# Mixer norms of a two-layer trunk: x turned by f32 matmuls with a diagonal of inverse roots, and first weights split in quarters

## The reference

```python
def rms_norm(x, gain):
    return x * lax.rsqrt(jnp.mean(x * x, axis=-1, keepdims=True) + EPS) * gain

for l in range(2):
    h = rms_norm(x, norm_mix[l])
    if l == 0:
        p = h @ even_w_in          # 1024 x 2560: u, v (gated), q, k, vv (attention)
        mix = concat(gated(u, v), stick_breaking(q, k, vv)) @ even_w_out
    else:
        mix = (B * conv3(C * hh)) @ odd_w_out    # B, C, hh: h @ odd_w_in, 1024 x 3072
    x = x + mix
    x = x + experts(rms_norm(x, norm_ffn[l]))    # 32 experts, 2 of them for each token
return rms_norm(x, norm_final)
```

## Time and profile before

| | |
|---|---|
| median of 3 runs | 1137.8 us (1137.17, 1137.8, 1138.01) |
| profiled execution | 1137.29 us, span 1135.5 us |
| busy: PE, DVE, ACT | 853.1 us (75%), 281.2 us (25%), 199.0 us (18%) |
| mean granted PE clock | 0.896 of full |
| DMA | 438.56 MB, 386 GB/s over the span |

### The profile page before, as it was taken

How to read it: one execution, slowest core, us unless ns; L and a number is a source line. 1 busy time by engine, 2 the same in 40 slices (tenths; PEclk the granted TensorE clock), 3 DMA queues, 4 the chain that set the end, 5 groups by cost and what they waited for, 6 DMA issues and landing times.

```text
span 1135.5 us, 29778 instructions
## 1 busy us (share of the span) xinstructions
PE 853.1 (75%) x13613; PEld 697.3 (61%) x13614; DVE 281.2 (25%) x692; ACT 199.0 (18%) x372; POOL 5.2 (0%) x31
## 2 busy tenths in 40 slices
PE   5999798576677676787679998876666776676874
PEld 5888776355555455565479987755554555554652
DVE  5666521011011010111157634110110110110211
ACT  5574310000000000000163331010000000000101
POOL 1000000000000000000000000000000000000000
PEclk9999899989798888889879997998998897888987
DMA  9953999999999999999996469999999999999995
GB/s 337 387 176 140 377 424 428 429 429 427 429 427 430 429 427 430 427 429 424 411 390 230 173 241 389 429 428 431 427 429 428 428 429 427 429 428 427 428 425 214
DMA packets 46075, 438.56 MB, mean 386 GB/s; under 512 B 5424, under 2 KB 6988, under 8 KB 20940
## 3 DMA queue, kind: packets, MB, share of 16 engines
q1 hardware_dynamic: 44444, 437.07, 92.4%
q10 hardware_dynamic: 1584, 0.79, 0.3%
HBM read 436.80 MB, written 1.05 MB: 386 GB/s over the span
## 4 chain that ended last, share of the span: by engine, by line
DMA 65%; PE 28%; DVE 3%; ACT 2%; issue 1%; SPq 0%; ACTq 0%; DVEq 0%
DMA ring<-in_w_gate 28%; DMA ring<-in_w_up 25%; PE psum L1134 9%; DMA ring<-in_w_down 8%; PE psum L1273 7%; PE psum L1166 4%; DMA ring<-in_odd_w_in 4%; PE psum L1305 2%; PE psum L1149 2%; PE psum L1280 2%; PE psum L1288 1%; ACT ring_halves L471 1%; DMA ring<-in_even_w_in 1%; PE psum L1345 1%; PE psum L1100 1%
## 5 line engine op out<-in xcount | busy, mean ns | idle before, releaser
L1273 PE MATMUL psum<-ring,m 128*32 128x128 f32 x7936 | 301.3, 316 | 205.4 <-DMA ring<-in_w_up 108.9
L1273 PEld LDWEIGHTS psum<-ring,m 128*32 128x32 f32 x7936 | 261.9, 127 | 250.9 <-DMA ring<-in_w_up 125.6
L1011 DVE TENSOR_TENSOR m<-psum,m 128x128 f32<-128x128 f32 x64 | 18.6, 291 | 602.0 <-ACT m L619 602.0
L1280 PE MATMUL psum<-ring,m 128*32 128x256 f32 x2048 | 129.4, 393 | 23.8 <-DMA ring<-in_w_down 23.6
L1134 PE MATMUL psum<-scr_halves,ring_halves 128*128 128x256 f32 x768 | 108.5, 289 | 4.3 <-DVE hn_halves L723 3.6
L1280 PEld LDWEIGHTS psum<-ring,m 128*32 128x32 f32 x2048 | 68.3, 111 | 64.2 <-issue 31.2
L619 ACT ACTIVATE m<-psum 128x128 f32<-128x128 f32 x64 | 17.8, 278 | 505.7 <-PE psum L1273 505.7
L1134 PEld LDWEIGHTS psum<-scr_halves,ring_halves 128*128 128x128 f32 x768 | 102.9, 198 | 5.2 <-DVE ring_halves L694 4.0
L1305 PE MATMUL psum<-m,hn 128*128 128x96 f32 x704 | 91.1, 292 | 12.6 <-ACT m L621 9.5
L1305 PEld LDWEIGHTS psum<-m,hn 128*128 128x128 f32 x704 | 87.5, 206 | 17.6 <-ACT m L621 14.2
L1288 PE MATMUL psum<-m 32*128 32x256 f32 x1056 | 89.2, 454 | 2.8 <-issue 1.9
(11 more groups left out here) (172 smaller groups left out, 477.9 us busy)
## 6 DMA issues: line engine op xcount, KB each, us to landing
ring<-in_w_down SPq DMA_DIRECT2D x64, 2048.0 KB, 39.8
ring<-in_w_gate SPq DMA_DIRECT2D x62, 2048.0 KB, 40.5
ring<-in_w_up SPq DMA_DIRECT2D x62, 2048.0 KB, 40.8
ring<-in_odd_w_in SPq DMA_DIRECT2D x6, 2048.0 KB, 20.5
ring<-in_even_w_in SPq DMA_DIRECT2D x4, 2048.0 KB, 16.6
ring<-in_even_w_out SPq DMA_DIRECT2D x2, 2048.0 KB, 19.7
ring<-in_odd_w_out SPq DMA_DIRECT2D x2, 2048.0 KB, 16.5
ring<-in_even_w_in SPq DMA_DIRECT2D x2, 1024.0 KB, 8.8
```

Of the source, the lines that this page charges most:

```text
L1273: last = pe.matmul(GU[CAP * part:CAP * (part + 1), lo:lo + FP], block_of(k), w_of(k)[:, FP * part:FP * (part + 1)], start=k == 0, stop=k = ...
L1280: last = pe.matmul(YB[CAP * part:CAP * (part + 1), 0:DP], hhT[:, CAP * f:CAP * (f + 1)], w[:, f, DP * part:DP * (part + 1)], start=f == 0, ...
```

## The change

The odd-numbered norms stay as they are, apart from the numbers in their waits. For n = 0 and 2:

- PE no longer transposes a scaled copy. It loads the 128 x 128 tiles of x itself as weights (reading every eighth element of a row of x), and multiplies them with a diagonal matrix that holds the tokens' inverse roots. 16 transposes become 16 ordinary f32 matmuls. They wait for both diagonals, and run in one sequence over j.
- The diagonals `rdiag` are made by DVE from the identity, one instruction each.
- At n = 2 ACT squares the sums straight from PSUM, in four pieces of 512 columns, while DVE copies them to x in two pieces. ACT reads banks 0 and 1 while DVE copies banks 2 and 3, then they change places. DVE adds the two part sums, and one root and one reciprocal serve both tiles.
- At n = 0 ACT squares tile 0 and DVE tile 1, with a row sum in the same instruction.
- The first weight of each mixer is loaded, rounded and multiplied in quarters of 1024 columns. ACT and DVE alternate: a quarter of the weight, then a pair of hT.
- ACT's preload of its root table comes ahead of its wait for the sums, where at n = 2 it came behind the first half weight.

The core of the diff:

```diff
+        rdiag = m[:, 2560:2560 + TT * P].rearrange("p (t c) -> p t c", t=TT)
+            def load_quarters(n, src):
+                for q in range(QUARTERS):
+                    ks = slice(2 * q, 2 * q + 2)
+                    sp.dma_start(wide(n)[:, ks, :], src[:, ks, :]).then_inc(first_landed[q], 16)
...
 scalar
+            def norm_even(n):
+                preload(ACT.Sqrt)
+                if n == 0:
+                    act.wait_ge(x_loaded[0], 16)
+                    act.activation(m[:, 0:D], x[:, 0, :], ACT.Square, accum_out=ssq[:, 0:1]).then_inc(norm_sums, 1)
+                    act.wait_ge(norm_sums, 1)
+                else:
+                    act.wait_ge(o_ready, TT + 1)
+                    for h in range(2):
+                        if h:
+                            act.wait_ge(x_ready, TT + 1)
+                        for t in range(TT):
+                            last = act.activation(m[:, 512 * (2 * h + t):512 * (2 * h + t + 1)].rearrange("p (c d) -> p c d", c=2),
+                                                  psum[:, 2 * h:2 * h + 2, DP * t:DP * (t + 1)], ACT.Square,
+                                                  accum_out=part_ssq[:, 2 * h + t:2 * h + t + 1])
+                        last.then_inc(norm_sums, 1)
+                act.wait_ge(norm_ssq, n // 2 + 1)
+                act.activation(ssq[:, :], ssq[:, :], ACT.Sqrt, bias=eps[:, 0:1], scale=1.0 / D).then_inc(norm_root, 1)
...
+                for j in range(4):
+                    weight_hi(L_ODD if n else L_EVEN, j)
+                    act.wait_ge(turned, 4 * n + j + 1)
+                    for kk in range(2):
+                        k = 2 * j + kk
+                        last = act.activation(hT_hi[:, k, :], bank[4 + j][:, kk * S:(kk + 1) * S], ACT.Copy,
+                                              scale=gains[:, n, k:k + 1])
+                    last.then_inc(hi_made, 1)
...
 vector
+            def norm_even(n):
+                if n == 0:
+                    dve.wait_ge(x_loaded[1], 16)
+                    link(dve.scalar_tensor_tensor(out=m[:, D:2 * D], in0=x[:, 1, :], scalar=1.0, in1=x[:, 1, :],
+                                                  op0=ALU.mult, op1=ALU.mult, accum_out=ssq[:, 1:2]))
+                    dve.wait_ge(norm_sums, 1)
+                    dve.sem_inc(norm_ssq, 1)
+                else:
+                    dve.wait_ge(o_ready, TT + 1)
+                    for h in (1, 0):
+                        if h == 0:
+                            dve.wait_ge(norm_sums, 2)
+                        dve.tensor_copy(x_flat[:, :].rearrange("p (t c d) -> p c t d", t=TT, c=NP)[:, 2 * h:2 * h + 2],
+                                        psum[:, 2 * h:2 * h + 2, :].rearrange("p c (t d) -> p c t d", t=TT)).then_inc(x_ready, 1)
+                    dve.wait_ge(norm_sums, 3)
+                    dve.tensor_tensor(ssq[:, :], part_ssq[:, 0:TT], part_ssq[:, TT:2 * TT], ALU.add).then_inc(norm_ssq, 1)
+                dve.wait_ge(norm_root, n // 2 + 1)
+                dve.reciprocal(rstd[:, :], ssq[:, :]).then_inc(norm_inv, 1)
+                dve.wait_ge(norm_inv, n // 2 + 1)
+                for t in range(TT):
+                    dve.tensor_scalar(rdiag[:, t, :], ident[:, :], rstd[:, t:t + 1], None, ALU.mult).then_inc(norm_diag, 1)
+                if n == 0:
+                    dve.wait_ge(smalls_loaded[0], 16)
+                    dve.wait_ge(smalls_loaded[1], 16)
+                    dve.wait_ge(turned, 4)
+                for j in range(4):
+                    weight_lo(L_ODD if n else L_EVEN, j)
+                    dve.wait_ge(hi_made, 2 * n + j + 1)
...
 tensor
+                if n % 2 == 0:
+                    if n == 0:
+                        for t in range(TT):
+                            pe.wait_ge(x_loaded[t], 16)
+                    pe.wait_ge(norm_diag, TT * (n // 2 + 1))
+                    for j in range(4):
+                        for kk in range(2):
+                            for t in range(TT):
+                                xk = x[:, t, :].rearrange("p (q k) -> p k q", k=K)[:, 2 * j + kk, :]
+                                last = pe.matmul(bank[4 + j][:, kk * S + t * P:kk * S + (t + 1) * P], xk, rdiag[:, t, :],
+                                                 start=True, stop=True)
+                        last.then_inc(turned, 1)
+                    return
...
-                for ks in ((range(HK), range(HK, K)) if first else (range(K),)):
+                for ks in ([range(2 * q, 2 * q + 2) for q in range(QUARTERS)] if first else (range(K),)):
                     if first:
-                        pe.wait_ge(w_lo, 2 * split_number(n) + ks[0] // HK + 1)
+                        pe.wait_ge(w_lo, split_count(n, ks[0] // 2))
+                        pe.wait_ge(lo_made, 4 * l + ks[0] // 2 + 1)
```

More of the change, by code:

```diff
@@ L168, in trunk @@
         gate_used, out_half = sem("gate_used"), sem("out_half")
-        first_landed = [sem(f"first_landed{i}") for i in range(2)]
+        first_landed = [sem(f"first_landed{i}") for i in range(QUARTERS)]
         early_landed = [sem(f"early_landed{i}") for i in range(2)]
@@ L251, in split_number, with is_first, split_count, split_whole @@
             return n - L_EVEN if n < L_MOE[0] else L_MOE[0] - L_EVEN + n - L_ODD
+        def is_first(n):
+            return n in (L_EVEN, L_ODD)
+        def split_count(n, part):
+            return 2 * split_number(n) + 2 * (n > L_EVEN) + 2 * (n > L_ODD) + part + 1
+        def split_whole(n):
+            return split_count(n, QUARTERS - 1 if is_first(n) else 1)
         def wait_landed(eng, n, turns=0):
-            eng.wait_ge(landed[n % RING], (turns + (n // RING + (n % RING > 0))) * 16)
+            apart = sum(n > z and n % RING == z % RING for z in APART)
+            eng.wait_ge(landed[n % RING], (turns + (n // RING + 1 - apart)) * 16)
         @contextmanager
@@ L381, in _ @@
                 if n == 0:
-                    for half in range(2):
-                        ks = slice(HK * half, HK * (half + 1))
-                        sp.dma_start(wide(L_EVEN)[:, ks, :], cols(even_w_in[0], c)[:, ks, :]).then_inc(first_landed[half], 16)
+                    load_quarters(L_EVEN, cols(even_w_in[0], c))
                     small_loads()
@@ L460, in preload, with weight_hi @@
                 preloads[0] += 1
[L462 to L466, removed]
+            def weight_hi(n, part):
+                parts = QUARTERS if is_first(n) else 2
+                c = slice(SLOT // parts * part, SLOT // parts * (part + 1))
+                if is_first(n):
+                    act.wait_ge(first_landed[part], 16 * (1 + (n == L_ODD)))
                 else:
@@ L494, in norm @@
                                ACT.Copy, scale=rstd[:, 1:2]).then_inc(hn_act, 1)
[L495 to L509, removed]
                 for j in (1, 3):
@@ L1060, in _ @@
             dve.wait_ge(consts_ready, 1)
-            for t in range(TT):
-                dve.wait_ge(x_loaded[t], 16)
             norm(0)
@@ L1091, in turn @@
                             last.then_inc(turned, 1)
[L1093 removed]
+                pe.wait_ge(hn_dve, TT * (n // 2) + 1)
                 turn(0)
[L1095 to L1103 removed]
+                pe.wait_ge(x_ready, TT * n)
+                for t in range(TT):
+                    for part in range(NP):
+                        pe.matmul(bank[part][:, DP * t:DP * (t + 1)], ident[:, :], x[:, t, DP * part:DP * (part + 1)],
+                                  start=t == 0, stop=False, skip_group_check=True)
+                pe.wait_ge(hn_dve, TT * (n // 2) + 2)
+                pe.wait_ge(hn_act, n // 2 + 1)
                 turn(1)
```

102 lines of the change are left out of this document (42 added, 60 removed).

## The result

The changed kernel took 1141.09 us (median of 9 runs, 1138.72 to 1141.64) against 1137.12 for the kernel before on the same chip (9 runs, 1135.75 to 1140.3). The ratio is 1.0033, 95% interval 1.0023 to 1.0043: slower by a third of a per cent. The profiled execution has a span of 1139.6 us, 4.1 more than before. The forecast was 3.8 less.

What follows compares the result with a forecast made beforehand. DMA was taken to bound the expert stages and PE the mixers, whose gains pass through whole. A gain of 4.0 at n=2 less 0.2 at the start gave 3.8 us off: median 1134.0, range 1131.5 to 1139.0.

Steps and rivals of the forecast that it cites:

- What bounds the kernel: Whole chain: DMA holds the expert stages, PE the mixers; a microsecond PE gains at a mixer's head reaches the end whole.
- The steps before PE: Squares, sums, root, reciprocal and diagonals at both even norms: PE starts at 8.65 at n=0 and 570.2 at n=2.
- The price of 16 turns: Both even norms: 0.43 us a turn cold, 0.234 warm; 16 cost 6.9 us cold, 3.7 warm, against about 3.9 before.
- a rival at 0.86 a turn: Step of 8 elements doubles weight loads at both even norms: 13.8 us per norm, total 1152; chance 0.08.
- The Trainium skill's factor of 4 for FP32: Turns at both even norms: 4 times a transpose's price, 15.6 us for 16; as a rival 1156, chance 0.01.
- The start: n=0: between a gain of 0.7 and a loss of 1.0, ends 1.5 and -2.1; a loss of 0.2 taken.
- My bad end: n=0 without a clock rise: first weight starts at 17.6, takes 13.6 us, ends at 31.2, a loss of 2.1.
- The unbroken run at the second place: n=2: PE runs without pause from 570.2, clock rises after 4.9 us, turns end at 576.2; gain 4.0 taken.
- clock not back in time: Rival, chance 0.20: turns don't raise the clock; first weight at n=2 takes 13.8 us, total 1138.0.
- The transposes brought no rise: Old n=2: transposes in two bursts with a pause left the clock unraised, while real matmuls raised it within 4.2 to 4.9 us.
- Quarters and queues: First weights in quarters: extra issues cost nothing; DVE and PE start after 1.15 us of weight work instead of 2.3.
- The cover that I named for the later loads: At the start: a 0.9 us delay is harmless, as a weight landed at 19.8, copied in 6.4, is needed at 28.4.

Runs made afterwards that it cites:

- experiment 9: Changed kernel without DVE's wait for all first-norm turns, plus dummy matmuls of 256 columns on PE ahead of the turns at both even norms: 1140.96 us, ratio 1.0035.
- Experiment 1: Changed kernel with turns reading contiguous 128-column tiles of x instead of every eighth element; channels permuted, routing differs: 1234.22 us, total not comparable.
- Experiment 3: Changed kernel without DVE's wait for all 16 turns at the first norm: 1135.73 us, ratio 0.9997 to the kernel before.
- experiment 5: Changed kernel with 16 small 28 x 28 transposes added on PE ahead of the first norm's turns: 1141.41 us, ratio 1.0043 to the kernel before.
- experiment 2: Changed kernel with the first norm back to squares on ACT, scaled copy and 16 transposes, quarters kept: 1131.74 us, repeated 1131.95.
- experiments 7: Changed kernel with scaled copies and transposes at both even norms, keeping quarters and squares from PSUM: 1130.72 us, ratio 0.995 to the kernel before.
- 10: Kernel with scaled copies and transposes at both even norms, PE at the second waiting for both copies and transposing pair by pair: 1129.49 us, ratio 0.9935.
- Experiments 6: Changed kernel with turns as strided transposes of x against the identity, roots left out, so routing differs: 1129.7 us, single run, total not comparable.
- experiment 8: Kernel with scaled copies and transposes at both even norms, plus dummy matmuls on PE ahead of them, four and eight: 1131.9 us, ratio 0.9956.

## Why the prediction was wrong

**What bounds the kernel: right.** Gains and losses at the mixers' heads came through to within 0.9 us at each step; the largest departure, 0.85, was mostly the router's clock.

**The steps before PE: right.** The two diagonals took 0.48 us (0.4 taken), DVE's square 1.23 (1.3), PE started at 8.59 (8.65) and 3.8 us after the sums (3.9).

**The price of 16 turns: the first step that failed.** I took 0.43 us a turn at half clock and 0.234 warm, "by the nearest rows". They cost 0.48 to 0.49 at both levels (7.88 us for 16 at the start, 7.67 wholly at full clock in experiment 9). The nearest rows had contiguous weights. Experiment 1 puts those at 0.43 and 0.22: my figures, had there been no step. I had the step only as a rival at 0.86 a turn, priced by ACT's ratio, and let it be hidden at half clock, which it nearly is; I did not ask what it does to the warm ones, where it is the price. At the second place that alone is 16 x 0.49 = 7.9 instead of 6.0 us. The rival's mechanism came true, not its size: the turns stay under the 0.5 us that was to show it and under the 0.55 from which it was to decide alone. The Trainium skill ("SBUF — State Buffer", section Door 1: The DMA port swizzle) has the penalty for crossing lines but no duration. Experiments 1 and 9 give one for a step of 8 elements, 0.03 us a record at half clock and 0.13 at full; that the lines are what makes it was not isolated, as no other step was run. The Trainium skill's factor of 4 for FP32 ("TensorE: Matmul & The Clock Gate", section Terms) is not what the runs show: at half clock 0.213 us for a transpose against 0.427 for an ordinary turn with contiguous weights, 2.0 times, and 0.480 with the step, 2.25 times.

**The start: the second step that failed.** I saw that DVE waits for all turns and took a loss of 0.2, between a gain of 0.7 and a loss of 1.0, with -2.1 as the worst. Measured -3.84. The turns ended at 16.5 instead of 14.6 (1.9, the step above); the pause was 2.4 as against 2.1; and the clock, full by then, fell in it, and brought the first weight to 14.16 us, 0.54 more than before. Experiment 3 shows that the wait and its clock are worth 4.9 us, more than the whole loss; this decided the sign. My bad end had the turns end at 15.5, the weight start at 17.6 and take 13.6; it started at 18.84 and took 14.16.

**The unbroken run at the second place: the third.** "PE runs without a pause from 570.2" is what failed: PE stopped for 2.1 us behind the third turn. With it the 3.9 us that are missing there are accounted for to within 0.1: 1.9 by the price of the turns, 2.1 by the pause. I let the clock rise 4.9 us after the first turn, and it rose 9.3 us after it (574.85 to 584.1); but that cost nothing, since the turns take the same at either level and the first weight, from 585.00 on, ran at full clock and was done 11.8 us later. So the rival "clock not back in time" did not happen there: its sign was a first weight of 13.6 us. The pause stood in no part of the prediction. Its cause is shown as far as this: PE waits for nothing there that the profile shows, instructions added far ahead move it (experiment 5), and another program length leaves it out (experiments 2, 7, 10). That it is the fetch of PE's instructions is argued from this and from the q8 packets, which each pause follows by the same 2.4 to 2.7 us; no run isolates it.

**An argument that was wrong without deciding.** "The transposes brought no rise", which I held for real matmuls. Experiments 6 and 10 speak for the pause between the bursts and not their kind: transposes with the weight's matmuls right behind them had the clock up 3.8 us after the first transpose. What helps at this norm is the order by pairs without a pause; in it the ordinary matmuls take 23.29 us and the scaled copies with transposes 20.91, though their PE starts 1.75 us later.

**Quarters and queues: right in sign, and larger.** I counted the quarters inside the turns' path; alone they are worth 2.6 us at the start (12.97 against 15.53, experiment 2). The cover that I named for the later loads, the second weight landing at 19.5 and rounded by 26, is thin: experiment 8 ran into it after 0.5 us.

**Two readings that were off, without weight.** The row at 12.31 in the earlier trace rows is DVE's lower half of the first half weight, not the rest of ACT's copy. And the gather's clock, at a mean of 0.62 in 135.5 to 136.0, rose at 135.9, so 5.2 us after its start and not 4.9.

What stays open: a transpose of x itself with the step at full clock was not seen, and no version gives the roots to such a transpose; with the roots left out the second norm took 19.74 us (experiment 6), 1.2 less than the best full version.

## What to carry to other kernels

When a cheap copy plus transpose is replaced by a matmul that reads the operand in place, price the weight load by its access and at both clock levels; a row at half clock hides what full clock will show. Then look at each gap of PE around it: a wait behind all of a loop's results, 2.2 us here, cost 2.65 more in clock. Even 0.65 us between transposes and weight went with a first weight some 1.5 us longer (experiments 7 and 10, one profile each). Test the parts alone, for here the quarters, the squares from PSUM and the order were worth 0.65% together, and the turns by ordinary matmuls, with the wait and the pause that came with them, took more than that away.

## What was not expected of the hardware

- Records of ordinary f32 matmuls whose 128 weight columns are read with a step of 8 elements start 0.24 us apart whatever clock is granted; with contiguous columns it is 0.213 at half and 0.112 at full.
- In transposes the same step cost nothing at half clock (0.213 us with and without).
- After the end of the first expert stage PE stood for 1.7 to 5.7 us with nothing to wait for in six of the versions with the usual routing, in different places for different programs, and each time until 2.4 to 2.7 us after a q8 packet had started.
